# Reordering the head of a hybrid decoder layer: two adaLN accumulators, latent tiles first, the rope and dt tile third

## The reference, cut to what matters

```
mod = c @ w_ada + b_ada                      # shift, scale, gate: 3 x 1024
u = x * (1.0 + scale) + shift
proj = u @ w_in                              # 1024 x 4304
q_lat, kv_lat, z_attn, xbc, dt_raw, z_ssm = split_last(proj, IN_SPLITS)
#  384   256+64  1024   1536    16    1024
o_attn = mla_branch(rms_norm(q_lat), rms_norm(c_kv), rope ...) * silu(z_attn)
o_ssm = ssd_branch(silu(conv(xbc)), softplus(dt_raw + dt_bias), z_ssm, ...)
mixed = concatenate([o_attn, o_ssm]) @ w_out
out = layer_norm(DEEPNORM_ALPHA * x + gate * mixed)
```

## Time and profile before

| | |
|---|---|
| median of 3 runs | 1017.5 us (1015.96 to 1018.6) |
| profiled execution, its own time | 1015.77 us |
| its span | 1014.0 us |
| PE busy | 943.4 us (93%) |
| DVE busy | 730.5 us (72%) |
| ACT busy | 431.8 us (43%) |
| POOL busy | 266.7 us (26%) |
| mean granted TensorE clock | 0.987 of full |

### The profile page before, as it was taken

The page is one execution under the profiler, slowest core; times in us unless marked ns, Lnnn a source line. Parts: engine busy times, 40 slices in busy tenths (PEclk is TensorE's granted clock), DMA queues, the critical chain, the costliest instruction groups (busy, mean ns, idle before and its releaser), DMA issues.

```text
span 1014.0 us, 13999 instructions
## 1 busy us (share of the span) xinstructions
PE 943.4 (93%) x4841; PEld 775.0 (76%) x4841; DVE 730.5 (72%) x1205; ACT 431.8 (43%) x679; POOL 266.7 (26%) x136
## 2 busy tenths in 40 slices
PE   2879999999999999999989999999999699999994
PEld 2668778888778887888778887888887577888883
DVE  5869799756777676667377867767777847548958
ACT  2462244434453455343555445445444424323422
POOL 3322121211221211221534424424432300001404
PEclk9899999999999999999999999999999889999998
DMA  9972214211132221233431431431421619743502
GB/s 281 277 268 59 63 42 145 61 43 41 42 104 83 94 92 61 84 103 109 140 120 55 138 110 42 150 109 41 150 83 41 228 50 350 265 153 128 210 29 83
DMA packets 106554, 119.90 MB, mean 118 GB/s; under 512 B 13109, under 2 KB 84886, under 8 KB 106518
## 3 DMA queue, kind: packets, MB, share of 16 engines
q1 hardware_dynamic: 106358, 118.90, 36.0%
q10 hardware_dynamic: 160, 0.52, 0.2%
HBM read 86.38 MB, written 27.79 MB: 113 GB/s over the span
## 4 chain that ended last, share of the span: by engine, by line
PE 68%; DVE 12%; issue 9%; ACT 6%; SPq 3%; POOL 1%; DMA 1%; DVEq 0%; ACTq 0%; POOLq 0%
PE bank L673 14%; PE bank L675 14%; PE bank L674 14%; PE bank L763 14%; DVE small L1568 2%; PE bank L793 1%; PE bank L834 1%; ACT prob L1224 1%; PE bank L795 1%; SPq L383 1%; DVE dec L1474 1%; PE bank L914 1%; PE bank L899 1%; PE bank L903 1%; PE bank L901 1%
## 5 line engine op out<-in xcount | busy, mean ns | idle before, releaser
L574 POOL TENSOR_TENSOR wl<-wraw,wh 128x1024 fp32r<-128x1024 f32 x32 | 78.5, 2454 | 216.0 <-ACT wh L1059 216.0
L673 PE MATMUL bank<-uh,wh 128*128 128x512 f32 x288 | 115.4, 401 | 6.7 <-ACT ost L1075 2.5
L674 PE MATMUL bank<-ul,wh 128*128 128x512 f32 x288 | 113.8, 395 | 0.0
L675 PE MATMUL bank<-uh,wl 128*128 128x512 f32 x288 | 113.5, 394 | 0.0
L673 PE MATMUL bank<-owh,mxh 128*128 128x512 f32 x256 | 102.4, 400 | 1.0 <-ACT rs L1244 0.9
L763 PE MATMUL bank<-uh,wh 128*128 128x512 f32 x256 | 103.2, 403 | 0.0
L763 PE MATMUL bank<-ul,wh 128*128 128x512 f32 x256 | 100.8, 394 | 0.0
L675 PE MATMUL bank<-owh,mxl 128*128 128x512 f32 x256 | 100.5, 393 | 0.0
L674 PE MATMUL bank<-owl,mxh 128*128 128x512 f32 x256 | 100.5, 393 | 0.0
L763 PE MATMUL bank<-uh,wl 128*128 128x512 f32 x256 | 100.1, 391 | 0.0
L1237 ACT ACTIVATE pth<-bank 128x512 fp32r<-128x512 f32 (+2 forms) x96 | 43.7, 492 | 74.8 <-PE bank L914 74.8
(11 more groups left out here) (221 smaller groups left out, 2280.6 us busy)
## 6 DMA issues: line engine op xcount, KB each, us to landing
wraw<-in_w_in SPq DMA_DIRECT2D x33, 512.0 KB, 3.7
owr<-in_w_out SPq DMA_DIRECT2D x32, 512.0 KB, 4.7
wada<-in_w_ada SPq DMA_DIRECT2D x16, 512.0 KB, 6.2
proj_scratch<-ost SPq DMA_DIRECT2D x16, 512.0 KB, 2.8
xin<-in_x SPq DMA_DIRECT2D x8, 512.0 KB, 6.0
cx<-in_w_ada SPq DMA_DIRECT2D x1, 4096.0 KB, 13.0
ssm_scratch<-xd SPq DMA_DIRECT2D x8, 512.0 KB, 3.5
tb<-ta SPq DMA_DIRECT2D x16, 256.0 KB, 3.7
```

What stands on the lines that cost most here:

```text
L574: pool.tensor_tensor(wl[:, p], wraw[:, p], wh[:, p].bitcast(F32), ALU.subtract).then_inc(w_split, 1)
L673: pe.matmul(dst, ah, bh, start=start, stop=False)
L674: pe.matmul(dst, ah, bl, start=False, stop=False)
L675: return pe.matmul(dst, al, bh, start=False, stop=stop)
```

## The change

What it does, in the order of the program:

- VectorE keeps two accumulators per k, for even and odd pieces; an instruction waits for the one two before it, and a ninth instruction adds the two (`two_sums`).
- All eight subtractions into `ul` are on VectorE, each behind the sum of the next k. For k = 7 ScalarE and VectorE work in two halves of 512.
- Tiles 0 and 1 are the first two latent tiles. The rope and dt tile is tile 2, in slots of its own (`wrx`, `whx`, `wlx`) and in PSUM banks 4 and 5.
- SP issues w_ada of a k ahead of x, weights of tiles 0 and 1 behind k = 0 and among k = 1, the rope and dt weights and the small inputs after everything of the eight k. ScalarE issues the six vectors.
- Tiles 3 to 7 are written out on TensorE instead of looped, and the two gate matmuls stand behind tile 6 instead of ahead of it.
- ScalarE makes `wh` of tile 3, copies tile 0 out, makes `wh` of tile 4 (which waits for `proj_ready` 6), copies tile 1 out, and then the dt rows.

```
 # VectorE
-                scaled_sum(acc[:, k % 2, :], lambda t, k=k: wada[:, k % 4, t, :]).then_inc(ada_acc, 1)
+            def two_sums(k):
+                dst = [acc[:, k % 2, a, :] for a in range(2)]
+                before = ch.n
+                for t in range(KT):
+                    w, a = wada[:, k % 4, t, :], t % 2
+                    if t < 2:
+                        ins = dve.tensor_scalar(dst[a], w, ccol[:, t:t + 1], None, ALU.mult)
+                    else:
+                        dve.wait_ge(dvec, before + t - 1)
+                        ins = dve.scalar_tensor_tensor(dst[a], w, ccol[:, t:t + 1], dst[a], ALU.mult, ALU.add)
+                    ins.then_inc(dvec, 1)
+                    ch.n += 1
+                dve.wait_ge(dvec, ch.n)
+                return dve.tensor_tensor(acc[:, k % 2, 2, :], dst[0], dst[1], ALU.add)
...
+                two_sums(k).then_inc(ada_acc, 1)
...
+                else:
+                    u_low(k - 1).then_inc(u_split, 1)
+            for n in range(NHALF):
+                u_low(KT - 1, slice(n * HB, (n + 1) * HB)).then_inc(u_split, 1)
...
 # SP
+            ada_columns(0)
+            x_columns(0)
+            sp.dma_start(wraw[:, 0], w3[:, :, 0:P]).then_inc(w_in_sem[0], 16)
+            ada_columns(1)
+            sp.dma_start(wraw[:, 1], w3[:, :, P:2 * P]).then_inc(w_in_sem[1], 16)
+            x_columns(1)
+            for k in range(2, KT):
+                ada_columns(k)
+                x_columns(k)
+            sp.dma_start(wrx[:, :, 0:ROPE], w3[:, :, W_KV_ROPE:W_KV_ROPE + ROPE]).then_inc(w_extra_in, 16)
+            sp.dma_start(wrx[:, :, ROPE:ROPE + 16], w3[:, :, W_DT:W_DT + 16]).then_inc(w_extra_in, 16)
+            small_inputs()
...
 # TensorE
+            pe.wait_ge(w_split, 3)
+            pe.wait_ge(uf_ready, KT + 1)
+            for n in range(NHALF):
+                for k in range(KT):
+                    r = slice(n * HB, (n + 1) * HB)
+                    mm = three(bk(4 + n), whx[:, k, :], wlx[:, k, :], uh[:, k, r], ul[:, k, r], k == 0, k == KT - 1)
+                mm.then_inc(proj_ready, 1)
+            proj_tile(1, 3)
+            for p in range(2):
+                proj_tile(p, 4 + p)
+            proj_tile(0, 6)
             pe.wait_ge(gate_acc, 1)
-            pe.wait_ge(uf_ready, KT)
+            pe.wait_ge(proj_evac, 6)
             for n in range(2):
                 mm = pe.matmul(bk(4 + n), ones[:], cx[:, 0, n * HB:(n + 1) * HB], start=True, stop=True)
             mm.then_inc(gate_mm, 1)
-            for p in range(2):
-                proj_tile(p, 6 + p)
+            proj_tile(1, 7)
...
 # ScalarE
-            high(0, 48, 2)
-            high(1, 32, 3)
+            high(1, 32, 3)
+            evac(0, 0, qk[:, 0, :])
+            high(0, 32, 4)
+            evac(1, 1, qk[:, 1, :])
             act.wait_ge(small_in, 16 * 11)
...
-            for t in range(2, 6):
+            for t in range(3, 6):
                 evac(t, t % 2, qk[:, t - 1, :])
```

More of the change, by code:

```diff
@@ L709, in _ @@
                     modulation(k + 1)
[L710 to L712 removed]
+                if k < KT - 1:
                     pe.wait_ge(u_split, k + 1)
[L714 to L732 removed]
+                    for p in range(2):
+                        if k == 0:
+                            pe.wait_ge(w_split, p + 1)
+                        for n in range(NHALF):
+                            proj_mm(p, n, k, k == 0, False)
+            for n in range(NHALF):
+                pe.wait_ge(u_split, KT + n)
+                proj_mm(0, n, KT - 1, False, True).then_inc(proj_ready, 1)
+            for n in range(NHALF):
+                proj_mm(1, n, KT - 1, False, True).then_inc(proj_ready, 1)
+            pe.wait_ge(w_split, 3)
+            pe.wait_ge(uf_ready, KT + 1)
+            for n in range(NHALF):
+                for k in range(KT):
+                    r = slice(n * HB, (n + 1) * HB)
+                    mm = three(bk(4 + n), whx[:, k, :], wlx[:, k, :], uh[:, k, r], ul[:, k, r], k == 0, k == KT - 1)
+                mm.then_inc(proj_ready, 1)
+            proj_tile(1, 3)
+            for p in range(2):
+                proj_tile(p, 4 + p)
+            proj_tile(0, 6)
             pe.wait_ge(gate_acc, 1)
[L735 removed]
+            pe.wait_ge(proj_evac, 6)
             for n in range(2):
@@ L1046, in _ @@
                     act.wait_ge(u_split, k - 1)
-                for dst in (uf[:, k % 2, :], uh[:, k, :]):
-                    m = act.activation(dst, bank[2][:].rearrange("p a b -> p (a b)"), ACT.Identity,
-                                       bias=modc[:, k:k + 1], scale=modc[:, 8 + k:9 + k])
-                m.then_inc(uf_ready, 1)
+                for r in ((slice(0, S),) if k < KT - 1 else (slice(0, HB), slice(HB, S))):
+                    for dst in (uf[:, k % 2, r], uh[:, k, r]):
+                        m = act.activation(dst, bank[2][:].rearrange("p a b -> p (a b)")[:, r], ACT.Identity,
+                                           bias=modc[:, k:k + 1], scale=modc[:, 8 + k:9 + k])
+                    m.then_inc(uf_ready, 1)
+                if k == KT - 2:
+                    act.wait_ge(w_extra_in, 32)
+                    act.activation(whx[:, :, 0:ROPE], wrx[:, :, 0:ROPE], ACT.Copy)
+                    act.activation(dt_columns(whx), wrx[:, :, ROPE:ROPE + 16].unsqueeze(2).to_broadcast([P, KT, 4, 16]),
+                                   ACT.Copy).then_inc(w_hi, 1)
             def high(p, arrived, tile):
@@ L1081, in _ @@
             act.activation(dtw[DT0:P], dtw[DT0:P], ACT.Ln, bias=1.0).then_inc(dt_log, 1)
-            for t in range(2, 6):
+            for t in range(3, 6):
                 evac(t, t % 2, qk[:, t - 1, :])
-                high(t % 2, 16 * (t // 2 + 2) + (16 if t % 2 == 0 else 0), t + 2)
+                high(t % 2, 16 * ((t + 2) // 2 + t % 2), t + 2)
                 if t == 3:
@@ L1388, in _ @@
             dve.wait_ge(dt_done, CHUNKS)
+            dve.wait_ge(proj_ready, 6)
             ch.link(dve.tensor_copy(ach[rows], twice))
```

89 lines of the change are left out of this document (39 added, 50 removed).

## The result

The changed kernel takes 1022.4 us, the median of 18 runs (1016.85 to 1025.12), beside 1015.8 us for the kernel before (18 runs). The ratio is 1.0057, with an interval of 1.0045 to 1.0068: slower by 5.8 us, or 6.6 by the medians. The forecast was 7.0 us more.

The account below looks back on a forecast made before the run. TensorE's head was taken as bound by transfers and VectorE's sums, with VectorE's list close behind. Tile 2 11.8 us sooner, but sums done 7.0 us later: 1015.77 + 7.0 = 1022.8 us (1024.5 on the median's scale), range 1016 to 1030.

Parts of the forecast that it names:

- Sum of a k: Head, VectorE: with two accumulators the sum of a k takes 3.5 us against 3.9.
- Rival 3: Slow head, chance 0.15: instructions of the two sums don't overlap, 5.4 us more, or rope weights come late; 1029.9 us.
- The start: Head: second weight tile comes at 16 us, VectorE's period is 4.75 us, tile 2 starts at 57.6 us, before 69.39.
- The stall before tile 3: After tile 2: TensorE waits 1.8 us for `wh` of tile 4 and tile 1's copy-out, on no path in the end.
- The list: VectorE, dt rows to angles: angles at tile 2's end + 41.85, tile 6 5.5 us later, TensorE idle for 13 us.
- The clock at tile 6: Tile 6, after TensorE's idle time: matmuls at half clock cost 2.4 us (2.1 to 2.8).
- The gate matmuls: Behind tile 6 they are on the path, 1.88 us before; VectorE's gate vector waits for them, 9 us longer.
- The squares: VectorE, behind the gate vector: 13.25 us with a GpSimd meeting of 2.1 in it; TensorE waits 2.3 us more.
- The sums done: TensorE's sums of squares end at tile 2's end + 79.55 = 148.2 us, before at 141.18: 7.0 us later.
- Nothing after tile 8: Behind the sums TensorE has hardly a gap, so the 7.0 us delay is neither made up nor added to.

Follow-up runs that it names:

- dt-first kernel: Changed kernel with ScalarE copying out tiles 0 and 1 and the dt rows before making `wh` of tile 4: 1020.45 us, 1.0050 of the kernel before.
- The combination: Changed kernel with gate matmuls ahead of tile 6, dt rows copied out first, Sin later, squares ahead of the key's rope: 1005.02 us, 0.9887 of the kernel before.
- 72 fillers: Changed kernel with 72 matmuls of 128x128 into a bank nobody reads, ahead of tile 6: 1024.12 us, 1.0067 of the kernel before.

## Why the prediction was right, point by point

- **Sum of a k.** Forecast 3.5 us, measured 3.44. The Trainium skill ("VectorE: DVE Perf Modes", The DRAIN you can't avoid) says that the next instruction doesn't start until the pipe is empty, and the prediction made 4.4 us of it. The same section adds that a next instruction that is not held starts earlier, which the prediction left out. The traces show overlap, 0.41 against 0.52 us from start to start in otherwise equal instructions, so here the link did cost time; the run with one accumulator shows the difference at the end of the head. Rival 3 fell with it.
- **The start.** The second weight tile was there when ScalarE made `wh` at 14.78, not at 16. VectorE's period was 4.49 us, not 4.75, and only one group of its instructions in the head paid for a meeting with GpSimd (the six of one sum took 4.54 us instead of 2.46). Tile 2 started at 54.54 instead of 57.6. This is the largest error before the sums, 3.05 us, on the favourable side.
- **The stall before tile 3.** Forecast 1.8 us, measured 1.84. It was said to be on no path, and the 11.0 us for which TensorE waits before tile 6 all the same bear that out. The `wh` and the copy-out that make the stall also hold up the dt rows, though, and the dt rows are on the path.
- **The list.** From E (tile 2's end, 65.6 here) to the Ln done: forecast 9.1, measured 9.0. To the end of the angles: 41.85 against 41.9. From there to tile 6: 5.5 against 5.48. Tile 6 at E + 47.35, measured E + 47.34. Its wait was 11.0 us, forecast 13; the 1.4 us lost at half clock in tile 3 shortened it. In the second trace, without that loss, it was 12.64.
- **The clock at tile 6.** Forecast 2.4 us, measured 1.5: 12.40 us from the start of tile 6 to the gate matmuls instead of 10.9. The term was taken from a place with 10 slow matmuls; here there were 6, in the dt-first kernel 13. So the range of the term, 2.1 to 2.8, was too narrow.
- **The gate matmuls.** Forecast a wait of VectorE of about 9 us, measured 8.26. Moved back, they gave 3.0 us of the milestone.
- **The squares.** One meeting with GpSimd cost 0.95 us (2.17 instead of 1.22 at 128.47) and not 2.1, so TensorE waited 1.4 us and not 2.3.
- **The sums done.** Forecast E + 79.55, measured E + 77.6, with the two sizes above in it. In absolute time 143.21 against the forecast 148.2: 3.05 from the head, 0.9 from the clock, 1.1 from the meeting.
- **Nothing after tile 8.** This step isn't borne out, and here the right total is partly luck. By the forecast the 7.0 us stand whole at the sums and nothing is added later. Measured, the two traces of the changed kernel are there only 2.0 to 3.9 us behind the two of the kernel before, and the ratio over all runs is 5.8 us. A milestone forecast too late and 2 to 4 us that were not in the sum made up for each other.

Where these 2 to 4 us are the traces don't settle. From the sums to the end the changed kernel took 871.8 and 874.8 us, the kernel before 872.8 and 874.2. The runs that were not traced say more. In the 18 executions of the changed kernel the time follows the mean granted clock: 1016.85 and 1017.99 us at 0.984 and 0.985, the ten executions above 1022 us at 0.977 to 0.979. The slope is 1.04 us for each 0.001, and 0.001 of 1020 us is 1.02 us, which is what half clock costs where TensorE has work all the time. The traced execution is at 0.984 and the median at 0.979, so some 5 of the 5.6 us between them are time at half clock. In which stages these executions had it isn't on record, and the slope is read from executions as they came, not from an experiment.

The traces show one place after the sums. In the three traces with the old head TensorE waits 0.31 to 0.50 us for `dec` before the last pair of rounds of the SSD stage, and one of the three has a short fall of the clock afterwards. In the ten with the new head this wait is 1.01 to 1.96 us in nine, and eight of the ten have one or two stretches of 6 to 8 matmuls at half clock in the next 30 us (the table's last column). From the sums to the end the ten take 874.8 us on average, the three 873.1. TensorE in the second trace of the changed kernel, in order of time:

```profile
503.34 0.77 PE L661 MATMUL bank<-qlh,hwh 128*128 128x512 f32 x1 [0.57 <-issue]
503.90 0.63 PE L662 MATMUL bank<-qll,hwh 128*128 128x512 f32 x1
504.33 0.63 PE L663 MATMUL bank<-qlh,hwl 128*128 128x512 f32 x1
```

Each stretch costs 0.2 us per matmul, 1.2 to 1.7 us, and the wait 0.5 to 1.6. From the sums to the first product of K and Q it was 371.5 and 371.7 us in the traces of the kernel before, 372.0 and 375.2 in those of the changed one; from there to the end 501.4 and 502.6 against 499.8 and 499.6, which gives it back. The longer wait goes back to ScalarE, which waits longer for the latents that come back from memory.

ScalarE in the kernel before:

```profile
488.03 1.06 ACT L1188 ACTIVATE qlh<-wraw 128x1024 fp32r<-128x1024 f32 x1 [1.58 <-DMA wraw<-proj_scratch]
```

and in the changed one:

```profile
490.77 1.06 ACT L1197 ACTIVATE qlh<-wraw 128x1024 fp32r<-128x1024 f32 x1 [2.26 <-DMA wraw<-proj_scratch]
```

The transfer is issued at 484.40 and used at 488.03 before, 3.63 us; after, at 486.44 and 490.77, 4.33. In the second traces it is 3.79 and 5.24. The change doesn't touch this transfer, and why it takes longer stays open. No run was made to undo it. The combination has the same late falls in one of its two traces, and its median is 10 us under that of before all the same.

## What to carry to other kernels

Before a head is shortened, follow every fixed list that the shortened stage starts, not only the engine that waited: here the list of VectorE began with the head's last tile, lasted longer than the tiles behind it, and took back 12 of 14.9 us. A new order of the lists was worth 1 us on the old head and, with the gate matmuls and the dt rows moved as well, 16 to 17 on the new one. A wait that is removed at one meeting of two lists comes back at the next (11 us before tile 6 became 14.6 before the sums) unless the work that the next meeting needs is pulled ahead of what it doesn't need.

## What the runs showed of the hardware that was not expected

- A wait of 1.84 us of TensorE was followed by 7 matmuls at half clock in one execution and one of 1.78 us by none in the next, of the same kernel; one of 2.72 us at the same place, with 72 fillers later on, by 14. Ten us of small float32 matmuls, a 2.79 us wait behind them, didn't keep the clock up either. The long wait before tile 6 (10.9 to 12.6 us in five traces) was always followed by a fall, of 6 to 13 matmuls.
- Executions of the changed kernel spread by 0.8% (1016.85 to 1025.12 us), and the slower ones are those with the lower granted clock (0.985 down to 0.977).
- A VectorE instruction that meets a GpSimd subtraction takes 0.95 to 2.2 us longer, whatever its own length: in the changed kernel the scan at 82.35 took 2.46 us, its neighbours 0.42.
- VectorE's scalar_tensor_tensor of 128x256 starts 0.41 us after the one before it when it waits for the one two before, and 0.52 when it waits for the one right before.
